# Hybrid decoder trunk: the low parts of the mixer's weight blocks made by an accumulating DMA instead of a VectorE subtraction

## What is computed

```python
for each of 2 layers:
    x += 0.5 * swiglu(rmsnorm(x))                       # 1024 -> 2 x 2816 -> 1024
    xn = rmsnorm(x)
    (mq, mk, mv, mo, gates, gq, gk, gv, gg, glr, lx, ly, mgate) = split(xn @ w_in)
    y_ml  = head_layernorm(mlstm(mq, mk, mv, ...)) * sigmoid(mo)      # 4 heads
    y_gla = head_rmsnorm(gla(gq, gk, gv, ...)) * silu(gg)             # 4 heads
    y_lru = rglru(causal_conv(lx)) * gelu(ly)                         # 8 blocks of 128
    x += (sigmoid(mgate) . (y_ml, y_gla, y_lru)) @ w_out
    x += 0.5 * swiglu(rmsnorm(x))
y = rmsnorm(x)
```

## Time and profile before

| | |
|---|---|
| median of 3 runs | 3034.41 us (3033.58 to 3038.2) |
| profiled execution, its own time | 3036.17 us |
| its span, first to last instruction | 3034.4 us |
| PE busy | 2960.5 us, 98% |
| DVE busy | 2275.1 us, 75% |
| ACT busy | 1344.6 us, 44% |
| POOL busy | 12.9 us |
| mean granted TensorE clock | 0.995 |
| mixer of the first layer in the span | about 406 to 1103 us |
| mixer of the second layer | about 1903 to 2601 us |

### The profile page before, as it was taken

The page is one execution under the profiler, slowest core; times in us unless marked ns, Lnnn a source line. Parts: engine busy times, 40 slices in busy tenths (PEclk is TensorE's granted clock), DMA queues, the critical chain, the costliest instruction groups (busy, mean ns, idle before and its releaser), DMA issues.

```text
span 3034.4 us, 59859 instructions
## 1 busy us (share of the span) xinstructions
PE 2960.5 (98%) x24960; PEld 2909.9 (96%) x24960; DVE 2275.1 (75%) x3371; ACT 1344.6 (44%) x1733; POOL 12.9 (0%) x36
## 2 busy tenths in 40 slices
PE   7999999999999999999999999999999999999997
PEld 7999999999999999999999999999999999999997
DVE  7685867778878878585785857776878888785765
ACT  5453532334335654363553635333333456453543
POOL 1000000000000000000000000000000000000000
PEclk9999999999999999999999999999999999999999
DMA  3322232333222222222222223233222222222322
GB/s 122 111 83 99 96 109 103 110 113 114 86 101 92 77 85 83 85 98 97 97 84 97 98 96 105 88 131 124 91 95 88 101 91 90 86 72 96 111 84 71
DMA packets 60151, 292.74 MB, mean 96 GB/s; under 512 B 9384, under 2 KB 12264, under 8 KB 32072
## 3 DMA queue, kind: packets, MB, share of 16 engines
q1 hardware_dynamic: 45344, 241.43, 23.5%
q10 hardware_dynamic: 13984, 48.48, 4.3%
q0 software_dynamic: 656, 0.52, 0.1%
HBM read 268.90 MB, written 21.50 MB: 96 GB/s over the span
## 4 chain that ended last, share of the span: by engine, by line
PE 83%; DVE 11%; ACT 3%; issue 2%; DMA 1%; DVEq 0%; ACTq 0%; POOL 0%; POOLq 0%
PE stream_b L476 24%; PE stream_a L476 23%; PE mix L537 11%; PE stream_b L537 7%; PE stream_a L537 5%; PE stream_a L614 5%; DVE wl L1436 1%; PE mix L899 1%; PE stream_b L620 1%; PE mix L735 1%; PE mix L675 1%; PE mix L819 1%; DVE wl L1515 1%; PE mix L656 1%; PE mix L738 1%
## 5 line engine op out<-in xcount | busy, mean ns | idle before, releaser
L1436 DVE TENSOR_TENSOR wl<-stage,wh 128x2048 fp32r<-128x2048 f32 (+1 forms) x148 | 332.8, 2249 | 88.3 <-ACT wh L959 64.0
L959 ACT ACTIVATE wh<-stage 128x2048 fp32r<-128x2048 f32 (+1 forms) x134 | 252.1, 1882 | 323.2 <-PE stream_b L476 227.5
L476 PE MATMUL stream_a<-xh,wh 128*128 128x272 f32 x1408 | 298.0, 293 | 21.4 <-DVE xl L1442 13.2
L476 PE MATMUL stream_b<-xh,wh 128*128 128x272 f32 x1408 | 303.1, 296 | 0.0
L476 PE MATMUL stream_a<-xl,wh 128*128 128x272 f32 x1408 | 292.4, 289 | 0.0
L476 PE MATMUL stream_a<-xh,wl 128*128 128x272 f32 x1408 | 291.9, 289 | 0.0
L476 PE MATMUL stream_b<-xl,wh 128*128 128x272 f32 x1408 | 291.6, 289 | 0.0
L476 PE MATMUL stream_b<-xh,wl 128*128 128x272 f32 x1408 | 290.8, 288 | 0.0
L476 PEld LDWEIGHTS stream_a<-xh,wh 128*128 128x128 f32 x1408 | 222.7, 189 | 25.7 <-DVE wl L1436 13.2
L476 PEld LDWEIGHTS stream_b<-xh,wh 128*128 128x128 f32 x1408 | 222.4, 189 | 7.3 <-issue 3.3
L476 PEld LDWEIGHTS stream_a<-xh,wl 128*128 128x128 f32 x1408 | 222.5, 190 | 0.0
(11 more groups left out here) (429 smaller groups left out, 8331.9 us busy)
## 6 DMA issues: line engine op xcount, KB each, us to landing
stage<-in_w_mix SPq DMA_DIRECT2D x88, 1024.0 KB, 4.9
stage<-in_w_up SPq DMA_DIRECT2D x87, 1024.0 KB, 4.8
stage<-in_w_down SPq DMA_DIRECT2D x16, 1024.0 KB, 5.0
stage<-in_w_down SPq DMA_DIRECT2D x32, 512.0 KB, 4.4
stage<-in_w_down SPq DMA_DIRECT2D x16, 768.0 KB, 4.5
CS<-in_c ACTq DMA_DIRECT2D x8, 1024.0 KB, 4.7
out_o_sc<-CS ACTq DMA_DIRECT2D x8, 1024.0 KB
CS<-in_s ACTq DMA_DIRECT2D x8, 1024.0 KB, 4.9
```

The source lines that it names most:

```text
L476: mm = [pe.matmul(out(h), a(h), b(h), start=f, stop=z) for h in range(2)]
L959: act.activation(wh[:, slot, 0:width], stage[:, slot, 0:width], ACT.Copy).then_inc(hi_done, 1)
L1436: tt_(wl[:, slot, 0:width], stage[:, slot, 0:width], wh[:, slot, 0:width].bitcast(F32), ALU.subtract).then_inc(split_done, 1)
```

## The change

For the 44 blocks of a layer that start with the mixer's third (blocks 2 to 43 and the first two of `w_out`, 88 in all), the low part is made in another way. ScalarE writes the negated rounded copy into `wl` first, and then the rounded copy into `wh`. GpSimd waits for the first of them, issues a DMA that adds `stage[slot]` onto `wl[slot]`, waits until it has landed, waits for `hi_done` and for the turn in `split_done`, and raises `split_done` with a one-column memset. VectorE's `split_lo` for these blocks is gone.

```diff
+        token = sb("token", [P, 1])
...
+        minus_high, lows_landed = sem("minus_high_parts"), sem("low_parts_landed")
...
                 ins.then_inc(xs_ready, 1)
+                for i in range(MIX_BLOCKS):
+                    n = L * LAYER_BLOCKS + BLK_MIX + 2 + i
+                    k, slot = L * MIX_BLOCKS + i, i % 2
+                    pool.wait_ge(minus_high, k + 1)
+                    pool.dma_start(wl[:, slot, :], stage[:, slot, :], accum_op=ALU.add).then_inc(lows_landed, 16)
+                    pool.wait_ge(lows_landed, k * 16 + 16)
+                    pool.wait_ge(hi_done, n + 1)
+                    pool.wait_ge(split_done, n + 2)
+                    pool.memset(token[:], 0.0).then_inc(split_done, 1)
...
-            def split_hi(nh, slot, through, width):
+            def split_hi(nh, slot, through, width, minus=False):
 
                 act.wait_ge(block_loaded[slot], nh * 16 + 16)
                 act.wait_ge(tile_done, through + 3)
+                if minus:
+                    act.activation(wl[:, slot, 0:width], stage[:, slot, 0:width], ACT.Copy,
+                                   scale=-1.0).then_inc(minus_high, 1)
                 act.activation(wh[:, slot, 0:width], stage[:, slot, 0:width], ACT.Copy).then_inc(hi_done, 1)
...
-                split_hi(nh + 1, 1, t + 3, 2 * D)
+                split_hi(nh + 1, 1, t + 3, 2 * D, minus=True)
...
-                split_lo(n + 4, 0, 2 * D)
...
-                split_lo(n + 5, 1, 2 * D)
...
+                        dve.wait_ge(split_done, L * LAYER_BLOCKS + i * 2 + (BLK_OUT + 4 + j))
                         split_lo(L * LAYER_BLOCKS + i * 2 + (BLK_OUT + 2 + j), j, 2 * D)
```

More of the change, by code:

```diff
@@ L1248, in mlstm_head @@
                 if not first:
-                    split_hi(nh + 1, 0, t + 1, 2 * D)
+                    split_hi(nh + 1, 0, t + 1, 2 * D, minus=True)
                 if not last:
@@ L1260, in mlstm_head @@
                 next(gates)
-                split_hi(nh + 2, 0, t + 5, 2 * D)
+                split_hi(nh + 2, 0, t + 5, 2 * D, minus=True)
                 next(gates)
@@ L1267, in mlstm_head @@
                 next(gates, None)
-                split_hi(nh + 2, 1, t + 7, 2 * D)
+                split_hi(nh + 2, 1, t + 7, 2 * D, minus=True)
                 act.wait_ge(head_samples, L * (8 * HEADS) + i * 4 + 5)
@@ L1348, in split @@
                 def split(b):
-                    split_hi(nh + (3 * j2 + b) // 2, (3 * j2 + b) % 2, t + 2 * b - 3, 2 * D)
+                    split_hi(nh + (3 * j2 + b) // 2, (3 * j2 + b) % 2, t + 2 * b - 3, 2 * D, minus=True)
                 split(2)
@@ L1366, in mix @@
                 ln_1p_exp_neg_abs(merged[0:HEADS, 6, :], merged[0:HEADS, 5, :], gate_ln)
-                split_hi(L * (LAYER_BLOCKS // 2) + BLK_MIX // 2 + 1, 0, L * LAYER_TILES + (TILE_MIX + GATE_TILES + 1), 2 * D)
+                split_hi(L * (LAYER_BLOCKS // 2) + BLK_MIX // 2 + 1, 0, L * LAYER_TILES + (TILE_MIX + GATE_TILES + 1), 2 * D, minus=True)
                 act.wait_ge(rows_ready, L + 1)
@@ L1773, in gate_rows @@
                 take(L * LAYER_TILES + (TILE_MIX + GATE_TILES + 1), 1, kT[:], DK ** -0.5)
-                split_lo(L * LAYER_BLOCKS + BLK_MIX + 2, 0, 2 * D)
             def take_values(t):
@@ L1899, in mlstm_head @@
                 if not first:
-                    split_lo(n + 2, 0, 2 * D)
                     take_values(t + 2)
@@ L1923, in mlstm_head @@
                     states(c, DV + 1, lambda c: SI[:, c * C + C - 1:(c + 1) * C], lambda c: c, a_u, a_c, B * NC)
-                split_lo(n + 3, 1, 2 * D)
                 if not first:
@@ L2152, in take_y @@
                     take(t + 2 + v, v, lyg[:, v, :])
-                def split(b):
-                    split_lo(n + b, (3 * j2 + b) % 2, 2 * D)
                 take_x(0)
@@ L2162, in lru_pair @@
                 take_x(1)
-                split(2)
                 conv(1)
@@ L2183, in lru_pair @@
                 take(t + 4, 0, br[:, 0])
-                split(3)
                 decayed(1)
@@ L2192, in lru_pair @@
                     lru_x(L, i + j2, 1 - j2, 0)
-                split(4)
                 return merge
```

## The result

The changed kernel takes 3043.34 us (median of 6 runs, 3040.86 to 3045.26), the kernel before 3035.49 us beside it (6 runs). The ratio is 1.0028, with a 95% interval of 1.0016 to 1.0039: slower by 0.3%, some 8 us. The side was right; the forecast was 3073.

A forecast was written before the change was run, and what follows sets the result against it. TensorE was taken as the bound, busy 2960.5 of 3034.4 us. A layer loses 23.2 - 3.9 = 19.3 us, two layers 38.6, giving 3073 us, 1.3% slower; the 8-in-10 range is 3027 to 3170, the forecast case's own 3040 to 3105.

The forecast's parts named there:

- Room and sequence: Each block's time from ScalarE's copy to TensorE's first matmul, 7.9 to 23 us, against a new sequence of 10.7 us.
- The DMA's 8.5 us: GpSimd's accumulating DMA: 1.7 + 6.2 = 7.9 us with two reads in sequence, plus 0.6 for software descriptors.
- the RG-LRU's loss: Block B of the last three RG-LRU pairs comes late by 2.5, 2.9 and 2.9 us, 8.3 a layer.
- The mLSTM's and GLA's: Lateness at blocks 5, 9, 13 (6.0 us), 17 (0.7) and 21, 25, 29, 33 (8.2) of a layer.
- rival 1: Quick DMA of 4.9 us fits every room: 3024 us; chance of faster 0.10, sequence inside 7 but above 6 us 0.12.
- The store's 2.0 us: A 1 MB state store issued during the DMA delays it by 2.0 us, making the sequence 12.7 us there.
- What VectorE gives back, 3.9: Per layer, shorter TensorE waits: GLA decays 2.4 us, first RG-LRU pair's convolution 1.1, second output block 0.4.
- TensorE's idle as the upper bound: TensorE idles 12.2 us of a 697 us mixer, so relieving VectorE gives back at most some 24 us in two layers.
- ScalarE's passes hidden: 44 extra ScalarE passes of 1.9 us, 84 us a layer, cost nothing; if RG-LRU cover fails, 11 us in all.
- Rivals 2 and 3: Three DMA passes in sequence, 11 us: 3133 us, chance 0.22; adder slower than transfer, 13 us: 3185 us, chance 0.14.
- Rival 4: One-input VectorE instructions hold up GpSimd's DMA descriptors: +10 us a layer, 3093 us, chance 0.05.
- SP's loads later "with 12 us of matmuls still to come": SP's loads start 6.5 us later, with 12 us of matmuls still ahead; no cost was charged.

## Why the prediction was right in its side and wrong in its size

- **Room and sequence, right.** TensorE waits for the token where the sequence exceeds the room, and taking those blocks from the DMA takes the waits away (the two runs with VectorE at tight blocks). The rooms themselves were read rightly: at 36 and 39 it was 8.0 without the wait, and the sequence of 9.4 put them 1.4 late.
- **The DMA's 8.5 us, the step that failed.** It is 6.93. The bounds, 4.9 and 11.0, held it; the value was too high because I charged the second read its full 3.1 us (2.8 measured, the addition included) on top of a base that was a load from HBM (4.9), where the copy within SBUF takes 4.13, and added 0.6 us for software descriptors that no run shows as a delay of the landing: the issue takes 0.85 instead of 0.53 us, inside the 6.93. The hops were too low by 0.3. So the sequence to TensorE's first matmul is 9.4 us, not 10.7.
- **What that alone does to the sum.** With 9.4 the RG-LRU's loss falls from 8.3 to 1.2 + 1.6 + 1.6 = 4.4 us a layer (5.4 measured in the first mixer, plus 1.6 at lower clock). The mLSTM's and GLA's falls from 14.9 to 0.7 or 0.8 at each of seven blocks, 5.0 in all. The output block's gain grows from 0.4 to 1.7, so VectorE gives back 5.2. Two layers then lose 2 x (4.4 + 5.0 - 5.2) = 8.4 us, and 7.9 were measured. That the two meet so closely is luck, since the other terms below were off too and cancel: over both mixers the ledger has 22.3 us lost where the prediction had 46.4, and 13.8 gained where it had 7.8.
- **The chances.** The Trainium skill, "DMA: Bandwidth & Descriptors", Anatomy of one DMA, gave an estimate of 6.8 for the DMA, and this trace agrees with its 6.93. The two-read rule of the Trainium skill, "Collectives: The Full Stack", Part 3, fits in kind: the DMA that reads twice takes 2.8 us more than the copy; that the addition itself costs nothing, no run shows. I took the rows' sum and not the Trainium skill's estimate, which was right. The case of a DMA between 6 and 7 us stood under rival 1 with a chance of 0.12 and a time within 6 us of no change; the measured 8 us lies just outside that. It lies inside the forecast's own range (3040 to 3105), though the DMA was just quicker than the 7 to 9.7 us of that case.
- **The store's 2.0 us, wrong.** It is 0.4 to 0.7 at blocks 5, 9, 13, 17, 25 and 29. What goes with a long DMA is a transfer issued ahead of it or just behind it: SP's load 0.9 us ahead (block 37 above) 3.3 us, the row load 1.9 ahead at block 10 2.5, the store 0.3 ahead at block 33 3.1 and 1.0 behind the start of GpSimd's issue at block 21 2.9 (737.35 and 736.31), where one 1.3 behind it (blocks 25 and 29) cost 0.7. The prediction had the right order of size for a shared DMA and put it at the blocks where the store comes 2.0 us behind. Blocks 10, 21 and 33 were late by this, 4.7 us in the first mixer. For the mLSTM and GLA blocks together the prediction had 14.9 us; these 4.7 are all that was lost there, and block 10 was one to which it gave nothing.
- **What VectorE gives back, 3.9, too small.** It is 8.0 in the first mixer and 5.8 in the second, where the gains at blocks 23 and 34 do not come. The two waits for the decays came as worked out (1.3 each). The 1.7 at block 23, a gap that the trace gives to no other engine, I had put down to TensorE itself; it goes with VectorE's instruction alone, in the run that cuts it to 16 columns. The rest is 0.8 at block 18, 0.5 more at the convolution (block 34) and 0.9 more at the output block.
- **TensorE's idle as the upper bound, too low.** "No relief can give back more than some 24 us" fell to the 29 measured. TensorE's idle time in the whole span did fall by 24 us only, from 73.9 to 50.0; but its busy time fell too, by 5.0 us from the earlier trace rows to the page of the run without subtraction:

```profile
PE 2955.5 (98%) x24960; PEld 2908.5 (97%) x24960; DVE 2080.1 (69%) x3283; ACT 1344.5 (45%) x1733; POOL 22.9 (1%) x124
```

  Matmuls at half clock count as busy. One such stretch of the kernel before lies behind a 2.1 us wait in the second mixer, with the clock as the last column but two. It is gone in the other run, and the one in the changed kernel cost 1.6 us, so it explains about a third of the 5.0. The rest may be the end of the matmul's row ahead of each wait, of which there are 41 before and 25 without the subtraction; that is argued, not shown:

```profile
2204.00:2216.00 12.00, 11.98 (x109) 11.23 (x110) 8.24 (x17) 2.46 (x2) 0.00 (x0) 0.86 0.04 13
```

- **ScalarE's passes hidden, right, and by the cover named.** Without VectorE's relief they cost 39 us, in more places than the three RG-LRU pairs named.
- **Rivals 2 and 3** fall with the 6.93 us. **Rival 4** wasn't tried apart; landings of 6.9 to 7.0 in all stretches without another transfer speak against it.
- **SP's loads later "with 12 us of matmuls still to come": a term put at nothing that was not.** It shows at block 3. From the kernel without the DMA to the changed one that block comes 2.7 us later in the first mixer and 3.0 in the second. The rows of the changed kernel are the first three, those without the DMA the last two:

```profile
428.35 0.09 POOL L476 MEMSET token<- 128x1 f32 x1 [6.52 <-DMA wl<-stage]
428.61 0.33 SPq L376 DMA_DIRECT2D stage<-in_w_mix  x1
429.50 0.45 ACTq L1242 DMA_DIRECT2D seven<-rows_scratch  x1
```

```profile
421.75 0.33 SPq L376 DMA_DIRECT2D stage<-in_w_mix  x1
427.84 0.44 ACTq L1240 DMA_DIRECT2D seven<-rows_scratch  x1
```

  The adding DMA has landed before the `seven` load is issued. But its token lets SP's load go only then, 0.9 us ahead of the `seven` load, which takes 6.2 us; without the DMA SP's load goes 6.1 us ahead of it, and it takes 4.1. In the kernel before the two also stand together (428.97 and 428.77, 6.8 us), and in the run with all tight blocks at VectorE as well (428.24 and 429.31, 7.2 us). So the late token takes back here what VectorE's relief had given.

What stays open: of the DMA's 35 us, 22 are the shifts at the blocks that wait for the token, the lower clock behind them included (12.5 in the first mixer, 9.7 in the second), and 5.7 lie at block 3. The rest is in the main in the second mixer: 3.0 at block 19, where a wait is followed by a stretch at lower clock, and 2.1 at block 34, where TensorE waits 1.75 us for ScalarE's `wri` load (6.4 us to its landing, 2.9 in the kernel before). That these loads are late by what is beside them is argued from such rows; no run moved one alone.

## What to carry to other kernels

Cost an operation that you move to another engine by the length of the chain to whoever waits, block by block, and not by busy shares: 88 passes of 1.9 us cost some 1 us in one chain and cost 39 us in another. A DMA's time alone is not enough: this one took 6.9 us alone and 9.5 to 10.0 at blocks 10, 21 and 33; list what is issued just ahead of it and within about a microsecond behind its start. Cutting the DMA into halves made the sequence 0.6 us shorter alone and 2.0 us longer beside a store (11.55 against 9.52 at block 5). And a mixed version that keeps the old path at the few tight blocks can be the better kernel: here 3031.7 us against 3036.5 and 3043.3.

## What the runs showed that I had not expected

- A DMA that adds keeps the 16 DMA engines about twice as long per byte as a copy: the middle one of its 8 KB packets takes 639 ns in the trace, that of the plain copy 332 and that of a store 309.
- The packets of two queues took two orders, both around block 5: a whole DMA held a later store back, and of two halves the second shared with it. Why, no run here shows.
- Behind the 2.10 us wait the granted clock was 0.86 over 12 us (70 matmuls). In the run with halves a 2.6 us wait was followed by a window at full clock:

```profile
956.40:968.40 12.00, 11.90 (x88) 11.59 (x89) 7.65 (x23) 8.61 (x9) 1.72 (x2) 1.00 0.94 220
```

What tells the two apart no run here shows.
